# Seven norm tiles of the first half in one row, ahead of the next pass's weights and convolutions

## The reference

```python
h = rms_norm(x, ffn_pre_g[l]) * (1.0 + scale2) + shift2
u = depthwise_conv_centred(h @ w_up[l], conv_w[l], conv_b[l])   # width 3, D_FF = 2816
a, bval = jnp.split(u, 2, axis=-1)
y = (jax.nn.gelu(a, approximate=True) * bval) @ w_down[l]
x = x + gate2 * rms_norm(y, ffn_post_g[l])
```

## Time and profile before

| what | value |
|---|---|
| median of 3 runs | 3314.31 us (3312.76 to 3317.01) |
| profiled execution, its own time | 3320.73 us |
| its span, first to last instruction | 3318.9 us |
| PE busy | 3149.7 us, 95% |
| DVE busy | 2409.3 us, 73% |
| ACT busy | 1269.9 us, 38% |
| mean granted TensorE clock | 0.978 |

### The profile page before, as it was taken

One profiled execution on the slowest core, in us unless ns is written; L12 is line 12 of the kernel. 1 busy time (PEld: TensorE's weight loads), 2 busy tenths in 40 slices (PEclk: granted clock), 3 DMA queues, 4 the chain that ended last, 5 costly groups with the idle time before them and its releaser, 6 DMA issues.

```text
span 3318.9 us, 35380 instructions
## 1 busy us (share of the span) xinstructions
PE 3149.7 (95%) x13945; PEld 2536.3 (76%) x13945; DVE 2409.3 (73%) x2666; ACT 1269.9 (38%) x1658; POOL 195.5 (6%) x287
## 2 busy tenths in 40 slices
PE   4899999997899999989999999999999899999997
PEld 4667777775788888867777888888888788888885
DVE  5559687774499999985665576776777577777767
ACT  4423211110699999953333422122223322212122
POOL 0001522441000000000000000000000000000000
PEclk8899999998999999999999999999999999999998
DMA  7643421223521112256677412212115211111113
GB/s 276 196 151 133 143 105 69 96 89 126 186 52 36 36 36 48 61 179 190 218 229 249 159 42 62 60 43 62 54 50 206 89 42 62 42 50 54 42 62 122
DMA packets 138485, 349.32 MB, mean 105 GB/s; under 512 B 27176, under 2 KB 36264, under 8 KB 133832
## 3 DMA queue, kind: packets, MB, share of 16 engines
q1 hardware_dynamic: 120720, 303.02, 28.8%
q10 hardware_dynamic: 12096, 25.17, 2.0%
q0 software_dynamic: 5504, 18.88, 1.5%
HBM read 249.56 MB, written 92.20 MB: 103 GB/s over the span
## 4 chain that ended last, share of the span: by engine, by line
PE 48%; DVE 4%; DMA 3%; ACT 1%; issue 1%; SPq 0%; ACTq 0%; DVEq 0%
PE second_ps_a L90 10%; PE second_ps_a L91 10%; PE second_ps_a L92 10%; PE second_ps_b L90 6%; PE second_ps_b L91 6%; PE second_ps_b L92 6%; DMA early_w_st<-in_w_branch 2%; DMA merge_st_b<-scratch_rec 1%; DVE second_y L2240 1%; DVE second_y L2258 0%; ACT merge_wb_hi L1741 0%; DVE merge_wb_lo L1805 0%; DVE second_y L2255 0%; DMA scratch_h<-merge_x 0%; DMA ffn_x<-scratch_x 0%
## 5 line engine op out<-in xcount | busy, mean ns | idle before, releaser
L2240 DVE TENSOR_TENSOR second_y<-second_y,second_ps_b 128x512 f32<-128x512 f32 x654 | 444.3, 687 | 207.5 <-PE second_ps_b L92 207.5
L90 PE MATMUL second_ps_a<-second_h_hi,up_wu_hi 128*128 128x512 f32 x1408 | 549.4, 390 | 4.3 <-DVE up_wu_lo L1989 4.3
L91 PE MATMUL second_ps_a<-second_h_lo,up_wu_hi 128*128 128x512 f32 x1408 | 549.1, 390 | 0.0
L92 PE MATMUL second_ps_a<-second_h_hi,up_wu_lo 128*128 128x512 f32 x1408 | 548.8, 390 | 0.0
L1344 DVE TENSOR_TENSOR att_prob_lo<-att_prob,att_prob_hi 128x1024 fp32r<-128x1024 f32 x256 | 309.8, 1220 | 25.7 <-ACT att_prob_hi L1310 24.5
L90 PEld LDWEIGHTS second_ps_a<-second_h_hi,up_wu_hi 128*128 128x128 f32 x1408 | 265.0, 188 | 60.2 <-DVE up_wu_lo L1989 5.2
L92 PEld LDWEIGHTS second_ps_a<-second_h_hi,up_wu_lo 128*128 128x128 f32 x1408 | 265.2, 188 | 55.2
L91 PEld LDWEIGHTS second_ps_a<-second_h_lo,up_wu_hi 128*128 128x128 f32 x1408 | 265.1, 188 | 54.9
L90 PE MATMUL proj_ps<-h_hi,proj_w_hi 128*128 128x512 f32 x704 | 292.7, 416 | 5.5 <-DVE proj_w_lo L811 5.5
L90 PE MATMUL second_ps_b<-ffn_wd_hi,ffn_g_hi 128*128 128x512 f32 x704 | 276.7, 393 | 20.6 <-ACT second_y L2158 11.5
L91 PE MATMUL second_ps_b<-ffn_wd_lo,ffn_g_hi 128*128 128x512 f32 x704 | 275.8, 392 | 0.0
(11 more groups left out here) (240 smaller groups left out, 5813.4 us busy)
## 6 DMA issues: line engine op xcount, KB each, us to landing
up_w_st<-in_w_up SPq DMA_DIRECT2D x88, 512.0 KB, 6.0
ffn_wd_st<-in_w_dn SPq DMA_DIRECT2D x44, 512.0 KB, 3.7
first_w_ada<-in_w_ada SPq DMA_DIRECT2D x32, 512.0 KB, 4.4
scratch_gates<-proj_out SPq DMA_DIRECT2D x64, 256.0 KB, 2.0
early_w_st<-in_w_branch SPq DMA_DIRECT2D x32, 512.0 KB, 5.9
merge_gate<-scratch_gates SPq DMA_DIRECT2D x64, 256.0 KB, 3.5
scratch_h<-merge_x ACTq DMA_DIRECT2D x48, 256.0 KB, 4.8
first_raw_lo<-in_w_ada SPq DMA_DIRECT2D x8, 1024.0 KB, 13.1
```

The costliest lines, as they stand in the source:

```text
L90: pe.matmul(out, w_hi, x_hi, start=first, stop=False)
L91: pe.matmul(out, w_hi, x_lo, start=False, stop=False)
L92: return pe.matmul(out, w_lo, x_hi, start=False, stop=last)
L2240: dve.tensor_tensor(at, at, ps_d[:, q % 4, :], ALU.add).then_inc(s_y, 1)
```

## The change

Three edits, all in pass NP of `feeding`. On DVE, `norm_tile` for all seven tiles stands at the pass's head; tiles 2 to 6 stood at its end. The low part of pass NP + 1's weights (j = 0) is made behind pass NP's first convolution, as in every other pass; in pass NP it stood ahead of it. On SP, `finish(0)` stands between the two blocks of pass NP + 1's up weights; it stood behind both.

```diff
@@ sync
             if i + 1 < NI:
-                for j in range(2):
-                    wu.load(sp, i + 1, j)
-            if i == NP:
-                finish(0)
+                wu.load(sp, i + 1, 0)
+                if i == NP:
+                    finish(0)
+                wu.load(sp, i + 1, 1)
@@ vector
             if i == NP:
                 dve.wait_ge(s_g2, 16)
-                for t in range(2):
+                for t in range(TILES[0]):
                     norm_tile(0, t)
-                wu.low_part(dve, i + 1, 0)
             convolve(i, 0)
-            if next_weights and i != NP:
+            if next_weights:
                 wu.low_part(dve, i + 1, 0)
@@ vector
-            if i == NP:
-                for t in range(2, TILES[0]):
-                    norm_tile(0, t)
```

## The result

| | before | after |
|---|---|---|
| median | 3317.01 us (3311.88 to 3321.2, 7 runs) | 3328.83 us (3321.51 to 3329.9, 7 runs) |
| ratio | | 1.0032 (95%: 1.0021 to 1.0042) |
| profiled execution, span | 3318.9 us | 3327.8 us |

The account below looks back on a forecast made before the run. PE, busy in 95% of the span, was taken as the bound. Its loss at the boundary, 11.65 + 2.99 = 14.64 us, would become 17.02 + 2.99 = 20.01: +5.4 us on 3314.31 gives 3319.7 us, range 3315.8 to 3323.0.

Parts of the forecast that it names:

- The bound and the chain: At the half boundary: PE, busy 95% of the span, waits 11.5 us for take_down behind loads queued after seven stores.
- The new wait: Head of pass NP+1: PE stands idle 17.0 us from 2552.73 us, a gap that didn't exist before.
- the convolution: Pass NP's first convolution, now ahead of the low part of pass NP+1's weights: 3.58 us directly on the path.
- the memory loop: Norm tiles 2, 4 and 6 on DVE: each x1 load waits for the tile two before; tile 6's add starts at 2563.75.
- S: Sum of the x1 load landings for tiles 4 and 6: 9.4 us, 4.7 each, bounds 8.1 to 11.1.
- from tile 6 to PE: From tile 6's add on DVE to PE's first matmul of pass NP+1: 1.15, 3.58 and 1.27 us, together 6.00 us.
- What is off the path: Pass NP+1's second weight block, issued behind all seven stores: low half ready near 2572.7, needed past 2580, 8 us to spare.
- The old wait as cover: At take_down(NP): with PE 20 us further back, the old 11.5 us wait is gone, with 0.4 us to spare.
- The clock term: Half-clock matmuls after PE's stop: 2.99 us lost before and after alike, or 1.3 us less after.
- how the sum was carried to the time: PE's loss of 14.64 us becomes 20.01; the +5.4 us goes whole onto the 3314.31 us median, giving 3319.7.
- The classes: Chances for the whole kernel's time: within 0.2% (6.6 us) 0.67, slower 0.28, faster 0.05.
- Rival 1: Slow x1 loads at tiles 2, 4, 6, 5.5 us each: +7.0 us, 3321.3, slower by more than 0.2%; chance 0.28.

Follow-up runs that it names:

- DVE's edit alone: The changed kernel with SP's list as before, both weight blocks of pass NP+1 ahead of the stores: ratio 1.0016, 3324.39 us.
- The experiment made for it: The kernel before with pass NP's first convolution moved ahead of the low part of pass NP+1's weights: ratio 0.9997, 3318.03 us.
- the later sets: The changed kernel measured twice more with no edit, against the kernel before: ratios 1.0016 and 1.0018, 3324.47 and 3325.0 us.
- loads_ahead_of_stores: The kernel before with SP's stores of tiles 2 to 6 put behind the loads of pass NP+2's up weights: ratio 0.9959, 3303.65 us.

## Why the prediction missed

- **The bound and the chain: right.** Taking five of the seven stores from in front of the loads takes PE's wait away with nothing else touched, at about the price that the chain gave (0.9956 expected, 0.9959 measured).
- **The new wait: right.** 17.0 us forecast, 17.1, 17.1, 17.0 measured. Its parts hold one by one: the convolution 3.6, the memory loop 3.9 (S = 9.72 for 9.4), from tile 6 to PE 5.99 us (6.00 forecast). Tile 5, for which the prediction saw little wait, waits 0.78 us; it isn't on the chain.
- **What is off the path: right.** The second weight block is split at 2572.80 us and nobody on PE waits for it; DVE's edit alone gives the same time, within the intervals.
- **The old wait as cover: right for the changed kernel**, whose wait for `take_down` is gone in all three traces. The experiment made for it settles nothing: ratio 0.9997 for a delay of 1.5 us, within an interval that reaches to +2.0 us, and a trace that is longer.
- **The clock term: mis-sized.** I took 2.99 us on both sides and allowed only the after side to be lower. Three traces of before have 2.04 on average, three of after 2.70: +0.66 us where the sum had nothing. In the other direction, the half clock after the 1.9 us stop at 2519 us cost 1.71, 1.70 and 0.10 us before and 0.11 in all three of after, 1.06 less on average. That stop is the same in both kernels, and in the other traces that have it it cost 0.11 once and 1.71 to 1.72 four times, with either order on DVE, so I count it as chance. The 5.2 us are then 5.6 of stops (17.21 for 11.62), +0.66 and -1.06; without the chance they would be 6.3. The prediction's "the rows agree (9 and 14)" was a misreading: these slow matmuls follow two different stops of one trace, and say nothing of two runs.
- **The step that failed: how the sum was carried to the time.** "The difference is one of waits and goes over as it is: 3319.7 us" put a difference of 5.4 us on a base of three runs, 3314.31, and the range had no term for either's scatter: it was made only of x1 landings and clock. The time came out 9.1 us above the forecast. 2.7 us of that are the base, whose seven runs beside the changed kernel have a median of 3317.01 (larger sets have 3317 to 3318). The other 6.4 us are a difference of 11.8 us between the medians for 5.4; the traces place 3.7 at the boundary and 4.4 ahead of it, and the later sets have 5.3 and 6.0 by their ratios, 6.4 and 8.1 by their medians. Executions of an unchanged program scatter here by some 11 us (3311.5 to 3322.8 in 35 runs). Traces scatter by 3.7 us ahead of the boundary for the kernel before (2514.8 to 2518.5) and by 8 us over all programs whose code up to there is the same (2514.7 to 2522.9). Even the sets that agree with the sum, 3324.5 and 3325.0 us, lie above my 3323.0.
- **The classes.** +5.4 us stood 1.2 us under the bound of 6.6. With a term of 0.66 missing and a scatter of set medians of 2 us or more, "within 0.2%" deserved little over half, not two thirds. The first set says slower by 0.32%, the next two 0.16 and 0.18%, with intervals up to 0.24 and 0.27%. Why the first is higher stays open; its trace places the excess ahead of the boundary, where nothing differs.
- **Rival 1** (slow x1 loads) didn't decide it: it wanted S over 10.66, and S was 9.72, 9.65 and 9.53 in the three traces.

## What to carry to other kernels

Work moved ahead of a wait on an engine that others wait for isn't free just because the old wait disappears: compare the two waits' ends, not their causes. Here the real lever was one queue over: loads that somebody needs stood behind stores that nobody waits for, on a queue that runs in order, and re-cutting that list alone gave some 14 us. And carry a difference to a median with the median's own uncertainty; three runs weren't enough for 0.2%.

## What the runs showed of the hardware that I had not expected

- The price of one and the same stop of PE scatters by a factor of two: 11.1 to 11.7 us of idle were followed by 1.47, 1.70 and 2.96 us of loss to half clock in three traces of one program. A stop of 1.9 us was followed by 0.10 to 0.11 us in five traces and by 1.70 to 1.72 in six, and by nothing in between.
- A 512 KB load of x1, issued behind a 512 KB store, took 4.0 to 4.4 us with 3.85 us between such pairs. Within the stores of the first half, at spacings of 2.7 to 4.1 us, it took 4.1 to 5.5 us in the six traces of the kernel before and the changed one; it took 6.91 once, in a program whose order of transfers had not changed, and 6.6 where two weight loads had gone out just ahead of it (`loads_ahead_of_stores`).
